# Eleven RMS norms of a two-block transformer kernel: GpSimd's power in place of a root and a reciprocal

## The reference, cut to what matters

```
def rmsnorm(x, g):
    xf = x.astype(jnp.float32)
    y = xf * lax.rsqrt(jnp.mean(xf * xf, axis=-1, keepdims=True) + EPS)
    return (y * g.astype(jnp.float32)).astype(x.dtype)

for l in range(DEPTH):
    h = rmsnorm(x, norm_pre[l, 0]) * (1.0 + sc1) + sh1
    y = swiglu(h, ffn_w_gate[l, 0], ffn_w_up[l, 0], ffn_w_down[l, 0])
    x = x + 0.5 * g1 * rmsnorm(y, norm_post[l, 0])
    h = rmsnorm(x, norm_pre[l, 1]) * (1.0 + sc2) + sh2
    y = hybrid_mixer(h, ...)
    x = x + g2 * rmsnorm(y, norm_post[l, 1])
    h = rmsnorm(x, norm_pre[l, 2]) * (1.0 + sc3) + sh3
    y = swiglu(h, ffn_w_gate[l, 1], ffn_w_up[l, 1], ffn_w_down[l, 1])
    x = x + 0.5 * g3 * rmsnorm(y, norm_post[l, 2])
```

## Time and profile before

| what | value |
|---|---|
| median of 3 runs | 3291.13 us (3288.71 to 3294.78) |
| profiled execution's own time | 3294.89 us |
| its span | 3292.9 us |
| mean granted TensorE clock | 0.988 |
| busy share PE, DVE, ACT, POOL | 95%, 70%, 49%, 18% |
| chain that ended last: PE, DMA, DVE, ACT, POOL | 82%, 5%, 4%, 3%, 2% |
| HBM traffic | 193 GB/s over the span |

### The profile page before, as it was taken

How to read it: one execution, slowest core, us unless ns; L and a number is a source line. 1 busy time by engine, 2 the same in 40 slices (tenths; PEclk the granted TensorE clock), 3 DMA queues, 4 the chain that set the end, 5 groups by cost and what they waited for, 6 DMA issues and landing times.

```text
span 3292.9 us, 61632 instructions
## 1 busy us (share of the span) xinstructions
PE 3143.2 (95%) x21286; PEld 2844.8 (86%) x21286; DVE 2299.4 (70%) x4242; ACT 1612.4 (49%) x3026; POOL 601.9 (18%) x644
## 2 busy tenths in 40 slices
PE   6998899999999999999999999999998999999998
PEld 5778899988887866899999888889988999998998
DVE  6649778877777345897887777777666767666654
ACT  1224468864444354345886444454454434435443
POOL 0106435520000100361554000000010000000000
PEclk9999999999999989999999999999999999999999
DMA  7634744358887322445445788867643775753354
GB/s 284 236 128 154 229 164 136 134 197 262 263 265 230 129 90 77 135 166 173 140 134 178 241 264 262 265 225 263 204 160 128 261 254 206 257 194 132 129 184 147
DMA packets 176620, 632.11 MB, mean 192 GB/s; under 512 B 23624, under 2 KB 23632, under 8 KB 175728
## 3 DMA queue, kind: packets, MB, share of 16 engines
q1 hardware_dynamic: 134416, 491.48, 44.3%
q0 software_dynamic: 42064, 139.07, 13.2%
q10 hardware_dynamic: 16, 0.01, 0.0%
HBM read 627.21 MB, written 9.50 MB: 193 GB/s over the span
## 4 chain that ended last, share of the span: by engine, by line
PE 82%; DMA 5%; DVE 4%; ACT 3%; POOL 2%; DVEq 1%; issue 1%; ACTq 0%; SPq 0%
PE ps L642 21%; PE ps L483 11%; PE ps L485 10%; PE ps L484 10%; PE ps L471 7%; DMA ring<-stream 5%; PE ps L621 2%; PE ps L623 2%; PE ps L518 2%; PE ps L622 2%; POOL unit_low L2267 2%; PE ps L1035 2%; PE ps L1034 2%; ACT unit_high L1121 1%; DVE unit_low L1560 1%
## 5 line engine op out<-in xcount | busy, mean ns | idle before, releaser
L1560 DVE TENSOR_TENSOR unit_low<-ring,unit_high 128x1024 fp32r<-128x1024 f32 x600 | 784.3, 1308 | 273.2 <-ACT unit_high L1121 265.1
L1121 ACT CAST unit_high<-ring 128x1024 fp32r<-128x1024 f32 x656 | 686.3, 1046 | 533.9 <-PE ps L485 270.7
L483 PE MATMUL ps<-expert_x_high,unit_high 128*128 128x256 f32 x1968 | 567.4, 288 | 33.5 <-POOL unit_low L2267 24.0
L484 PE MATMUL ps<-expert_x_low,unit_high 128*128 128x256 f32 x1968 | 551.6, 280 | 0.0
L485 PE MATMUL ps<-expert_x_high,unit_low 128*128 128x256 f32 x1968 | 550.0, 279 | 0.0
L485 PE MATMUL ps<-norm_parts,unit_low 128*128 128x256 f32 x1504 | 424.2, 282 | 0.0
L483 PEld LDWEIGHTS ps<-expert_x_high,unit_high 128*128 128x128 f32 x1968 | 372.2, 189 | 44.8 <-POOL unit_low L2267 24.0
L485 PEld LDWEIGHTS ps<-expert_x_high,unit_low 128*128 128x128 f32 x1968 | 370.0, 188 | 0.0
L484 PEld LDWEIGHTS ps<-expert_x_low,unit_high 128*128 128x128 f32 x1968 | 369.9, 188 | 0.0
L642 PE MATMUL ps<-unit_high,expert_high 128*128 128x512 f32 x1024 | 320.3, 394 | 6.8 <-ACT expert_high L1496 6.8
L642 PE MATMUL ps<-unit_low,expert_high 128*128 128x512 f32 x1024 | 324.9, 398 | 0.4 <-DVE unit_low L1560 0.3
(11 more groups left out here) (322 smaller groups left out, 6704.6 us busy)
## 6 DMA issues: line engine op xcount, KB each, us to landing
ring<-stream SPq DMA_DIRECT2D x914, 512.0 KB, 3.5
score<-ada POOLq DMA_DIRECT2D x128, 512.0 KB, 5.3
arena<-ada POOLq DMA_DIRECT2D x96, 512.0 KB, 4.9
arena<-bias_tiles POOLq DMA_DIRECT2D x48, 192.0 KB, 2.7
arena<-ada SPq DMA_DIRECT2D x8, 1024.0 KB, 17.3
bias_tiles<-bias_rows POOLq DMA_DIRECT2D x8, 768.0 KB, 18.3
x_home<-x POOLq DMA_DIRECT2D x2, 1024.0 KB, 6.2
x<-x_home POOLq DMA_DIRECT2D x2, 1024.0 KB, 7.6
```

What stands on the lines that cost most here:

```text
L483: pe.matmul(out, hi[:, kt, :], xh[:, kt, :], start=(kt == 0), stop=False)
L484: pe.matmul(out, hi[:, kt, :], xl[:, kt, :], start=False, stop=False)
L1121: nc.scalar.copy(hi, ring[:, unit % SLOTS, :]).then_inc(whi_ready, 1)
L1560: V.tensor_tensor(out=lo, in0=ring[:, unit % SLOTS, :], in1=hi, op=ALU.subtract).then_inc(wlo_ready, 1)
```

## The change

The eleven late norms get their factor in another way. ScalarE writes sum / 1024 + eps with Identity in place of Sqrt into the same `stat[:, 0]`. GpSimd waits for `std_ready`, raises it elementwise to the power held in a column of `small`, -0.5, spread over the tile with stride 0, writes `stat[:, 1]`, and counts a new semaphore `rstd_ready` up. VectorE waits for that and multiplies; its reciprocal goes, and for an output norm the drain behind it. The Sqrt table is no longer asked for ahead of an output norm. On GpSimd `root` stands ahead of the phase's DMAs for an input norm and behind them for an output norm. Norms 0 to 4, the head norms and the group norms in hyb stay as they are.

```diff
@@ scalar
                 act.wait_ge(ss_ready, no + 1)
-                nc.scalar.activation(stat[:, 0], ps[0][:, 0:S], ACT.Sqrt, bias=eps, scale=1.0 / D).then_inc(std_ready, 1)
+                root = ACT.Sqrt if no <= 4 else ACT.Identity
+                nc.scalar.activation(stat[:, 0], ps[0][:, 0:S], root, bias=eps, scale=1.0 / D).then_inc(std_ready, 1)
@@ scalar, norm_out
-                have(ACT.Sqrt)
...
-                nc.scalar.activation(stat[:, 0], ps[0][:, 0:S], ACT.Sqrt, bias=eps, scale=1.0 / D).then_inc(std_ready, 1)
+                nc.scalar.activation(stat[:, 0], ps[0][:, 0:S], ACT.Identity, bias=eps, scale=1.0 / D).then_inc(std_ready, 1)
@@ vector, norm_in
                 if ph != "mix0":
-                    dve.wait_ge(std_ready, norm_no[ph] + 1)
-                    V.reciprocal(stat[:, 1], stat[:, 0])
+                    if norm_no[ph] > 4:
+                        dve.wait_ge(rstd_ready, norm_no[ph] - 4)
+                    else:
+                        dve.wait_ge(std_ready, norm_no[ph] + 1)
+                        V.reciprocal(stat[:, 1], stat[:, 0])
                 dve.drain()
@@ vector, add_normed
                 pair_squares(norm_no[ph] + 1)
-                dve.wait_ge(std_ready, norm_no[ph] + 2)
-                V.reciprocal(stat[:, 1], stat[:, 0])
-                dve.drain()
+                dve.wait_ge(rstd_ready, norm_no[ph] - 3)
@@ vector, start
+            V.memset(small[:, 31:32], -0.5)
@@ gpsimd
+            def root(no):
+
+                pool.wait_ge(std_ready, no + 1)
+                G.tensor_tensor(out=stat[:, 1], in0=stat[:, 0], in1=small[:, 31:32].to_broadcast([P, S]), op=ALU.pow).then_inc(rstd_ready, 1)
+
             for ph in phases:
+                if norm_no[ph] > 4:
+                    root(norm_no[ph])
                 if ph == "mix0":
...
                 elif ph != "ffn3":
                     ffn(ph, int(ph[-1]))
+                if norm_no[ph] >= 4:
+                    root(norm_no[ph] + 1)
```

More of the change, by code:

```diff
@@ L311, in program @@
         std_ready = sem("std_ready")
+        rstd_ready = sem("rstd_ready")
         mid_ready = sem("mid_ready")
```

## The result

The changed kernel takes 3742.47 us (median of 4 runs, 3741.24 to 3743.79) against 3292.95 us for the kernel before (4 runs): 449.5 us more, a ratio of 1.137 with a 95% interval of 1.1352 to 1.1388. The interval is 445 to 457 us more. The direction was forecast, the size was not: 42 us were expected, and the time lies far above the range that ended at 3425.

A forecast was written before the change was run, and what follows sets the result against it. The kernel was taken as TensorE-bound, each norm a pure sum of latencies. Eleven longer gaps, +35.6 us, plus 6.2 for TensorE's clock gave about +42: 3333 us on the median of 3291.13, range 3279 to 3425.

The forecast's parts named there:

- X: Time of one GpSimd power of 128x256 at each late norm, taken as 4.9 us, between 0.52 and 10.4.
- the third rival: The power is a chain of forty dependent steps, 20.8 us each norm; kernel 3513 us; chance 0.13.
- some 20: Plain steps assumed for a software power on GpSimd, each at most a full pass of 0.52 us: 10.4 us.
- The way by VectorE's reciprocal: Power as logarithm and exponential, each 4.1 plain operations at GpSimd's 0.52 us pass, plus a product: 4.8 us.
- The sum: Eleven norms' longer gaps, +35.6 us, plus 6.2 for TensorE's clock: about +42 us.
- the first rival: The power costs little more than a multiply, 0.6 to 1.0 us; kernel 7 to 11 us less, 3281; chance 0.24.
- TensorE's clock: TensorE slows after longer idle time at the norms: 5 x 1.24 = 6.2 us, bounds 0 and 12.4.
- my 1.24: Cost in us of one idle wait: eight sum products took 3.25 us after 4.00 us without work, 2.01 elsewhere.
- The hops: Engine handovers at each late norm: 0.08 us into GpSimd and about 0.12 us out of it.
- Identity for Sqrt and the table loads: ScalarE's changed activation keeps its 0.47 us and the saved 1.283 us table loads were hidden: worth 0.
- The moved DMAs: DMAs now queued behind GpSimd's power in input norms stay hidden; a rival had them late, 3343 us, chance 0.03.

The follow-up runs named there:

- The multiply: Changed kernel with GpSimd multiplying by a column of 0.001 in place of raising to the power; 3275.04 us on 3287.65, ratio 0.9970.
- the fillers: Changed kernel with 182 filler products in place of 13 around each late norm on TensorE; 3725.23 us on 3291.36, ratio 1.1335.

## Why the prediction was wrong, step by step

**The power's duration.** This is the step that failed: "I take X = 4.9 us", with 10.4 as its upper end. It was 41.13, 8.4 times the value and 4 times the bound; even the third rival, 20.8, lay at half of it. The lower end came from a row and held. The upper one did not come from a row at all: the pass of 0.52 us did, the "some 20" steps were a guess, and 41.13 / 0.52 = 79 passes were needed. The way by VectorE's reciprocal carried a ratio of 4.1, measured on one engine for one function, over to another function on another engine, for which nothing in the trace stood. The Trainium skill's GPSIMD Engine Reference (Performance pitfalls for Q7 kernels), at 4 cycles an element for a dependent step, gave 17 us for my 20 steps. The trace shows 160.7 ns an element, by the 1.2 GHz that this page of the Trainium skill gives (Specifications) an estimate of 193 cycles or 48 such steps; whether the power is a chain of that kind no run here shows. Shown is that the cost is the power's own, linear in the elements and the same for two exponents; what GpSimd does in this time stays open.

**The sum.** With the measured X the prediction's own formula, 11 x (X - 1.66), gives 11 x 39.47 = 434.2, and the eleven gaps are 433.5. The form was right: a norm is a sum of latencies, nothing covers it, break-even at 1.66 us. The multiply at 0.61 us was on the other side of this point and was faster, as the first rival's mechanism says.

**The range.** Its upper end does not come out of its own terms: X = 12 gives 11 x 10.34 = 113.7, with 12.4 for the clock 3417 on 3291, not 3425. It makes no difference to the outcome.

**TensorE's clock.** I took 6.2 us with 12.4 as the upper bound; measured are 12 to 24, and the traces show 20.2. There are two reasons. Every one of ten waits now has the idle time, where I had counted five. And a place costs more than my 1.24: from the 200th product on the five phases are 2.2 to 2.9 us behind. I had also called the loss in the output norms mostly hidden. It is not: the sums of norm 6 took from 2408.13 to 2415.12, 7.0 us against 5.8, since at half clock they fall behind the squares. The size was off; the mechanism is shown by the fillers.

**The hops.** 0.08 us into GpSimd as read; out of it 0.02, not 0.12. 1 us in all.

**What was worth nothing.** Identity for Sqrt and the table loads: 0 as forecast, by the run with them alone. The moved DMAs: ffn2's first four units go out at 2978.13 and the first is used at 2999.48 with no wait; hyb0's row goes out at 2456.75 and its first product, at 2466.09, stands in the chain with no wait ahead of it; ffn1's first four ada units go out at 2681.01, after the power, and the first is used at 2703.38 with no wait (GpSimd and VectorE, timeline of the kernel after):

```profile
2681.01 2.17 POOL L2379 DMA_DIRECT2D arena<-ada  x4
```

```profile
2703.38 1.22 DVE L1705 CUSTOM_DVE_ANT_0 arena<-arena 128x1024 f32<-128x1024 f32 x1
```

**The chances.** Slower had 0.66, and the direction was right, but 0.50 of it stood on an X that was 8 times too small; rival 3, which asked for over 12 us in the power and had 0.13, was the nearest. Since nothing bounded X from above, the range should not have stopped at a number that rested on a count of steps.

## What to carry to other kernels

An operation that no row of the trace shows has a lower bound from its neighbours on the same engine, and here it had no upper one: measure one of it alone, at a small size and at a large one, before it goes into a chain. On GpSimd a power costs 0.33 us a call and 0.16 us for each element of a partition. An estimate from these two for 2 columns is 0.65 us; at 8 columns it is the 1.6 us that this chain had to give, and a tile of 256 is far beyond. Where the factor of a norm is on the chain, look first for one activation that gives it, and then at which table load it leaves late. Whether another engine takes the power, and in what time, was not tried.

## What the runs showed of the hardware

- GpSimd's tensor_tensor with op pow: 41.13 us for 128x256, 20.73 for 128x128, 2.91 for 128x16; the same form with mult 0.61 us, 67 times less. Exponents -0.5 and -1 cost the same.
- TensorE's granted clock is 0.50 when work comes after 40 us without any. In the changed kernel it stays there from 2408 to 2412 and is 0.99 in the next 2 us; one such place costs 1.0 to 2.9 us. After 4.0 us without work it cost 1.24 us on eight passes, so a wait ten times as long is not ten times as dear.
- Fillers hold the clock as long as they last: 372 passes in 41.70 us at a granted clock of 1.00. Behind them and 2.3 us of idle time, sixteen products took 5.38 us in hyb0 and 3.69 in hyb1, the time of the kernel before.
- Abs_reciprocal_sqrt takes 0.474 us for 128x256 out of PSUM, Sqrt and Identity 0.473.
